# Modulation rounds laid out by column group, and one-pass spreading of the mLSTM maxima, in a two-layer DiT block

## The reference

```
s_lat, s_ctx = silu(c), silu(c_ctx)
for l in (0, 1):                                   # the six modulation vectors of each layer
    mod_lat, mod_ctx = s_lat @ ada_w[l] + ada_b[l], s_ctx @ ada_w[l] + ada_b[l]   # 1024 -> 6144
    h = rms_norm(x, g) * (1 + scale) + shift       # before the mixer and before the network
    x = x + gate * mixer(h); x = x + gate2 * swiglu(h2)
...
# mLSTM, in chunks of 128 tokens, per head and direction:
m_q = max(b + m, rowmax(dmat))                     # a stabilising maximum per query
p   = exp(dmat - m_q[:, None]) * (q @ k.T);  inter = exp(b + m - m_q)
h   = (inter * (q @ S) + p @ v) / max(abs(den), exp(-m_q))
```

## Time and profile before

| | us |
|---|---|
| median of three runs | 1793.11 (1791.22 to 1794.06) |
| the profiled execution | 1791.71 |
| its span, first to last instruction | 1789.9 |
| TensorE busy in the span | 1702.0 (95%) |
| DVE, ACT, POOL busy | 802.6 (45%), 591.5 (33%), 68.2 (4%) |
| mean granted TensorE clock | 0.98 of full speed |

### The profile page before, as it was taken

One profiled execution on the slowest core, in us unless ns is written; L12 is line 12 of the kernel. 1 busy time (PEld: TensorE's weight loads), 2 busy tenths in 40 slices (PEclk: granted clock), 3 DMA queues, 4 the chain that ended last, 5 costly groups with the idle time before them and its releaser, 6 DMA issues.

```text
span 1789.9 us, 26602 instructions
## 1 busy us (share of the span) xinstructions
PE 1702.0 (95%) x10524; PEld 1408.0 (79%) x10524; DVE 802.6 (45%) x1192; ACT 591.5 (33%) x1021; POOL 68.2 (4%) x116
## 2 busy tenths in 40 slices
PE   5999999889899999999999988999998899999998
PEld 4888878668788888888888866777776688888886
DVE  4687777433522222222222455666654533333333
ACT  4344444442421111121112333454664322222221
POOL 0321011000000000000000000000000000000000
PEclk8999999899999999999999998999999999999999
DMA  8532333122122431215221531101113233323233
GB/s 331 60 94 95 130 119 109 50 78 60 46 61 68 166 128 59 68 61 200 94 69 60 207 136 36 47 28 45 36 59 106 70 101 99 94 94 102 91 100 117
DMA packets 47219, 168.99 MB, mean 94 GB/s; under 512 B 5296, under 2 KB 5552, under 8 KB 47024
## 3 DMA queue, kind: packets, MB, share of 16 engines
q1 hardware_dynamic: 31408, 115.47, 19.9%
q10 hardware_dynamic: 14976, 51.52, 7.9%
q0 software_dynamic: 768, 1.08, 0.8%
HBM read 163.82 MB, written 4.19 MB: 94 GB/s over the span
## 4 chain that ended last, share of the span: by engine, by line
PE 88%; ACT 3%; DVE 3%; DMA 3%; issue 1%; ACTq 0%; SPq 0%; DVEq 0%
PE PS L472 52%; PE PS L1842 9%; PE PS L2030 7%; DMA scr<-in_ada 3%; PE PS L1719 3%; PE PS L1885 2%; PE PS L1728 2%; PE PS L1901 1%; PE PS L2118 1%; PE PS L2117 1%; PE PS L1735 1%; PE PS L1781 1%; PE PS L1867 1%; PE PS L1985 1%; PE PS L1795 1%
## 5 line engine op out<-in xcount | busy, mean ns | idle before, releaser
L458 DVE TENSOR_TENSOR w_lo<-raw,w_hi 128x1024 fp32r<-128x1024 f32 x196 | 239.8, 1224 | 254.2 <-ACT w_hi L453 248.5
L472 PE MATMUL PS<-h_hi,w_hi 128*128 128x512 f32 x1008 | 303.8, 355 | 2.6 <-DVE w_lo L458 2.6
L472 PE MATMUL PS<-h_lo,w_hi 128*128 128x512 f32 x1008 | 302.1, 354 | 0.0
L472 PE MATMUL PS<-h_hi,w_lo 128*128 128x512 f32 x1008 | 302.1, 354 | 0.0
L453 ACT ACTIVATE w_hi<-raw 128x1024 fp32r<-128x1024 f32 x196 | 206.3, 1053 | 262.6 <-PE PS L472 218.4
L472 PE MATMUL PS<-c_hi,w_hi 128*128 128x512 f32 (+1 forms) x672 | 204.5, 358 | 4.7 <-DVE w_lo L458 4.7
L472 PE MATMUL PS<-c_hi,w_lo 128*128 128x512 f32 (+1 forms) x672 | 201.9, 354 | 0.0
L472 PE MATMUL PS<-c_lo,w_hi 128*128 128x512 f32 (+1 forms) x672 | 201.7, 354 | 0.0
L472 PEld LDWEIGHTS PS<-h_hi,w_hi 128*128 128x128 f32 x1008 | 165.2, 188 | 30.7 <-DVE w_lo L458 3.3
L472 PEld LDWEIGHTS PS<-h_lo,w_hi 128*128 128x128 f32 x1008 | 165.8, 188 | 28.8
L472 PEld LDWEIGHTS PS<-h_hi,w_lo 128*128 128x128 f32 x1008 | 164.8, 188 | 28.0
(11 more groups left out here) (284 smaller groups left out, 2125.6 us busy)
## 6 DMA issues: line engine op xcount, KB each, us to landing
raw<-in_w SPq DMA_DIRECT2D x196, 512.0 KB, 3.5
scr<-in_ada ACTq DMA_DIRECT2D x48, 512.0 KB, 5.7
adaw<-in_ada ACTq DMA_DIRECT2D x32, 512.0 KB, 4.4
scr<-in_ada SPq DMA_DIRECT2D x8, 1024.0 KB, 10.1
X<-in_xT SPq DMA_DIRECT2D x4, 768.0 KB, 6.8
X<-in_xT ACTq DMA_DIRECT2D x1, 3072.0 KB, 10.2
x_spill<-X ACTq DMA_DIRECT2D x1, 2048.0 KB, 9.3
X<-x_spill ACTq DMA_DIRECT2D x1, 2048.0 KB, 10.0
```

What stands on the lines that cost most here:

```text
L458: nc.vector.tensor_tensor(w_lo[:, j], raw[:, j].rearrange("p (k n) -> p k n", k=KT), w_hi[:, j].bitcast(f32), ALU.subtract).then_inc(s_lo, 1)
L472: last = nc.tensor.matmul(G[j][:, a:b], w[:, j, k], m[:, k, a:b], start=(n == 1), stop=(n == 3 * k_tiles))
```

## The change

The first part is for the rounds of four chunks alone. `ada_four` turns the layout over: chunk q goes to column group q with all its eight input blocks, so the sum over the blocks is finished in PSUM, and a round fills 128 columns of a bank in place of 512. The four chunks take turns matmul by matmul, the input block is the outer loop. ACT copies 128 columns. `ada_turned` is a single f32 matmul: the copied block is the stationary operand, and eight columns of the identity (two of each group of 32) are the moving one. There are 32 matmuls in a round as before.

The second part is the maxima. POOL now rounds `rsel` to `fp32r` (rows 0 to 47 of `rs_r`) and writes the remainder into rows 64 to 111; the rows between are zero. A block of ones with 112 rows, rounded once, is the stationary operand of one `fp32r` matmul of 512 columns, which adds high and low part. The two new tiles lie in columns of `c_hi` and `c_lo` that the second layer doesn't use.

```diff
-        adr_f, at = carve(scr, at, 512)
-        adr_0 = scr[:, 8192:9216].rearrange("p (a n) -> p a n", a=2)
+        adr_f, at = carve(scr, at, 128)
+        adr_0 = scr[:, 8192:8448].rearrange("p (a n) -> p a n", a=2)
...
+        rs_r, ones_r = c_lo[0:112, 6:8, 512:768], c_hi[0:112, 7, 536:664]
...
+            nc.gpsimd.memset(rs_r.bitcast(f32), 0.0).then_inc(s_ones, 1)
+            nc.gpsimd.tensor_copy(ones_r, ones[0:112]).then_inc(s_ones, 1)
+            pool.wait_ge(s_ones, 2)
...
                 nc.gpsimd.tensor_tensor(rsel[0:48].rearrange("p (c i) -> p c i", c=CH), row, pick, ALU.mult)\
-                    .then_inc(s_rs2, 1)
+                    .then_inc(s_rsf, 1)
+                pool.wait_ge(s_rsf, 2 * n + 1)
+                whole = rsel[0:48].rearrange("p (a i) -> p a i", a=2)
+                nc.gpsimd.tensor_copy(rs_r[0:48], whole).then_inc(s_rsf, 1)
+                pool.wait_ge(s_rsf, 2 * n + 2)
+                nc.gpsimd.tensor_tensor(rs_r[64:112], whole, rs_r[0:48].bitcast(f32), ALU.subtract).then_inc(s_rs2, 1)
...
-                    nc.scalar.activation(adr_f, PS[:, 4], ACT.Copy).then_inc(s_adr, 1)
+                    nc.scalar.activation(adr_f, PS[:, 4, 0:128], ACT.Copy).then_inc(s_adr, 1)
...
+            def ada_four(ws, bank):
+                for k in range(KT):
+                    for q, w in enumerate(ws):
+                        last = MM(PS[32 * q:32 * q + 32, bank, 0:128], sT[:, k], w[:, 128 * k:128 * k + 128],
+                                  start=(k == 0), stop=(k == KT - 1))
+                last.then_inc(s_adm, 4)
+
+            def ada_turned(adr, dst):
+                pick = ident.rearrange("p (g r) -> p g r", g=4)[:, :, 0:2]
+                MM(dst.rearrange("p (g s) -> p g s", g=4), adr, pick, start=True, stop=True).then_inc(s_ads, 1)
...
                                 for q in range(4):
                                     pe.wait_ge(s_adf[q], 16 * na + 16)
-                                    ada_row(adaf[:, q], 4, q)
+                                ada_four([adaf[:, q] for q in range(4)], 4)
...
-                                ada_sums(adr_f, ADQ)
+                                ada_turned(adr_f, ADQ)
...
-                MM(PS[:, 5], ones[0:48, :], rsel[0:48], start=True, stop=True).then_inc(s_R, 1)
+                MM(PS[:, 5].rearrange("p (a i) -> p a i", a=2), ones_r, rs_r, start=True, stop=True).then_inc(s_R, 1)
```

More of the change, by code:

```diff
@@ L337, in program @@
         s_gw, s_wgh, s_wgl, s_g1, s_g2 = sem("gatew_loaded"), sem("gatew_hi"), sem("gatew_lo"), sem("gate_pe"), sem("gate_dve")
-        s_g3, s_fn = sem("gate_act"), sem("forget_negated")
+        s_g3, s_fn, s_ones, s_rsf = sem("gate_act"), sem("forget_negated"), sem("ones_rounded"), sem("rsel_step")
         s_pad, s_mcv, s_sil, s_rot, s_rope = sem("padded"), sem("mconv_step"), sem("silu_ready"), sem("rot_done"), sem("rope_step")
@@ L697, in _ @@
                     act.wait_ge(s_ads, n - 1)
-                nc.scalar.activation(adr_0[:, n % 2], PS[:, 6 + n % 2], ACT.Copy).then_inc(s_adr, 1)
+                nc.scalar.activation(adr_0[:, n % 2], PS[:, 6 + n % 2, 0:128], ACT.Copy).then_inc(s_adr, 1)
                 if n == 0:
@@ L1730, in ada_row, with ada_sums @@
                 last.then_inc(s_adm, 1)
-            def ada_sums(adr, dst, nq=4):
-                for q in range(nq):
+            def ada_sums(adr, dst):
+                for q in range(2):
                     last = MM(dst[:, 2 * q:2 * q + 2], adr[:, 128 * q:128 * q + 128], cn("fold"), start=True, stop=True)
                 last.then_inc(s_ads, 1)
+            def ada_four(ws, bank):
[7 more added lines that the diff above has]
+                MM(dst.rearrange("p (g s) -> p g s", g=4), adr, pick, start=True, stop=True).then_inc(s_ads, 1)
             def ffn(layer):
@@ L1818, in _ @@
                     pe.wait_ge(s_adr, n - 1)
-                for q in range(4):
-                    ada_row(scr[:, 1024 * (4 * (n % 2) + q):1024 * (4 * (n % 2) + q) + 1024], 6 + n % 2, q)
+                ada_four([scr[:, 1024 * (4 * (n % 2) + q):1024 * (4 * (n % 2) + q) + 1024] for q in range(4)], 6 + n % 2)
                 if n == 0:
@@ L1825, in _ @@
                 pe.wait_ge(s_adr, n + 1)
-                ada_sums(adr_0[:, n % 2], ADP[n])
+                ada_turned(adr_0[:, n % 2], ADP[n])
                 if n:
@@ L1953, in _ @@
                     pe.wait_ge(s_adr, 4 + U)
-                    ada_sums(adr_m, ADM, 2)
+                    ada_sums(adr_m, ADM)
                 if U < ADA_R:
```

## The result

The changed kernel is slower: 1801.28 us median of nine runs (1795.67 to 1806.96) against 1793.62 for the kernel before (nine runs, 1785.81 to 1794.91), a ratio of 1.0049 with a 95% interval of [1.0035, 1.0063]. By the ratio that is 8.8 us more (the two medians lie 7.7 apart). It is above the range given and near the slow rival (B), though only part of that rival's reason was at work. The profiled execution has a span of 1802.4 us.

A forecast was written before the change was run, and what follows sets the result against it. TensorE was taken as the bound, except in group 2, bound by the loop through the loads. Terms +7.4 + 5.5 - 4.9 - 0.9 - 9.1 + 0.6 (mLSTM clock) = -1.4 gave 1791.7 us, range 1784.5 to 1798.0.

The forecast's parts named there:

- rival (B): Layer 0, group 2: its loop runs cold, every round drops the clock, maxima gain only 5.8; +7.6 us, 1800.7, chance 0.13.
- The waits for four loads: Six late network rounds: all 32 matmuls follow the fourth load's landing, each ending 1.24 us later; +7.4 us.
- The clock behind them: Late network rounds: TensorE idles before the landing and its granted clock falls, 2.7 drops of 2.05 us; +5.5 us.
- The sums: Network rounds: four f32 matmuls become one, saving 0.59 us each, eight on the path in groups 0 and 1; -4.9 us.
- The copy: Start, rounds 1 to 3: ACT's copy of 128 columns, not 512, saves 0.31 us each; -0.9 us.
- The maxima: mLSTM: one fp32r matmul for the f32 one saves 0.65 us at 14 places; -9.1 us.
- POOL: mLSTM: three POOL instructions per unit end in time for TensorE; slowing of DVE put at 0, dear end +3 us.
- The sum: Whole kernel: all terms together give -1.4 us, 1791.7 us against the median; chance 0.44 within about 3 us.

The follow-up runs named there:

- the waits by themselves: Kernel before, changed only so TensorE waits for all four loads of a network round ahead of the first chunk: 1.0043, +7.7 us.
- The version with the waits removed: Kernel before plus column-group rounds, one turning matmul and ACT issuing group 2's next loads earlier; old maxima: 0.9994, -1.1 us.
- The part as a whole: Kernel before with only the new maxima (POOL rounds and subtracts, one fp32r matmul), rounds as before: 1.0004, +0.7 us.
- without POOL's added instructions: Kernel before with the short fp32r maxima matmul, high and low rows formed once and stacked, one POOL instruction per unit: 0.9979, -3.8 us.
- the version with two: Kernel before plus column-group rounds, earlier group 2 loads and the turning matmul issued twice in network rounds; old maxima: 0.9975.
- POOL's work by itself: Kernel before plus all POOL instructions of the new maxima, TensorE keeping the old f32 matmul: 1.0007, +1.3 us.
- the stacked maxima: Kernel before with one fp32r maxima matmul on high and low rows formed once, masked by one POOL instruction per unit: 0.9979, -3.8 us.

## Why the prediction was wrong, step by step

- **The waits for four loads** (+7.4): right in place, number and kind. Six rounds start in one run behind a landing, and the waits by themselves cost 7.7 us, clock included. In that profile the four rounds of group 2 are 4.4 us longer without the clock's share, 1.1 for each, where 1.24 was forecast.
- **The clock behind them** (+5.5, 2.7 drops): too large. In these rounds one drop showed in the changed kernel and two with the waits alone. Both had one behind the 3.5 to 4 us in the first round of group 2, the other was in the first round of group 0, behind 1.9 us; the nine other stretches, of 1.0 to 2.3 us, cost none. Round 4 was forecast to idle 3.1 us and to drop with 0.8; it idled 2.23 and didn't. Over all profiles in which a round waits in this way, the first round of group 2 idled 3.5 to 4.3 us and the clock fell behind 8 of 10; of the 34 other stretches, 0.6 to 2.5 us, it fell behind 4, each of 1.9 us or more. I had also stretched what the Trainium skill says (TensorE: Matmul & The Clock Gate, HAM oscillation): the kernel of that section waits about 3 to 5 us for a DMA before each burst, and here only the first round of group 2 does. (Four drops would be 1.5 more than the 2.5 put down for this group, not 1.3.) Together the first two terms were 12.9 and measured 7.7, in a kernel whose waits in group 2 are some 0.5 us shorter than those of the change.
- **The sums** (-4.9): the step that failed. Their own saving was under-sized if anything, 0.67 us each. But I took the products around them as fixed, and one f32 matmul in place of four put these at the slow pace: +7.8 us by the pairs. Sum and pace together are about +2 and not -4.9. The traces agree: from the first round of group 0 to that of group 2 TensorE's work at full clock is 388.6 us before and 389.5 in the changed kernel, where -4.7 was forecast. The version with the waits removed shows it too: it should have been some 6 us faster than before, and was 1.1.
- **The copy** (-0.9): where it was said to be, and near its size. From the end of a round's rows to the product behind it 2.91 us pass before and 2.58 in the changed kernel, in the third and the fourth round. The copy is shorter by 0.32 (0.28 in place of 0.60), so nothing of this comes from the shorter sums. The first whole projection begins at 62.5 us in the changed kernel and at 63.9 in the one before, and at 62.2 and 63.8 in the mean of the ten profiles with the new rounds at the start and of the seven without; what is beyond three times 0.32 isn't the copy. In the two profiles the clock also comes back earlier under the first product, which lasts 5.9 us in place of 7.0 (from 31.09 and from 30.73 us).
- **The maxima** (-9.1): the other step that failed, by more us, and in two ways. The saving was over-sized: 0.65 us at 14 places, from one pair of rows, where TensorE's work fell by about 6 us in all, as in half of the units the f32 maxima had been interleaved with the matmuls behind it. The rest was eaten by what I put at 0, **POOL** beside DVE. The part as a whole is at +0.7, and without POOL's added instructions at -3.8, so these take about 4.5 back (the two intervals overlap slightly). In the traces 1.9 of it is the one wait at the first outputs. The rest would be clock: over their runs the three kernels with these instructions and the short matmul have a mean granted clock of 0.975 to 0.976, all other versions 0.977 to 0.980; that this comes from the wait isn't shown. I had looked whether POOL ends in time for TensorE, and it does; I had not looked at what DVE does at that moment, which was the last thing ahead of the first outputs, with less than 1 us to spare before. The Trainium skill (GPSIMD Engine Reference, Key points) has this rule, that POOL contends with DVE instructions on two SBUF inputs; the trace agrees, with 1.53 us for one of 0.68.
- **The sum**: +7.7 for the waits, +7.8 for the pace, -6 for nine sums on the path (eight in groups 0 and 1 and the last), -1.4 at the start and +0.7 for the maxima make +8.8. That this meets the measured number to the tenth is luck, as the measured terms are known to 2 or 3 us each. The forecast of -1.4 had the two large gains without what each did to its neighbours. Rival (B) gave 1800.7, near the time, by five clock drops in these rounds of which one came in the profile; it was right by accident.

What stays open: why the parity of f32 matmuls between the products (whether their number is odd or even) sets the pace. Each is two records with two weight loads in the trace, so it isn't the parity of records; the median weight load takes 188 ns at either pace. Products of 512 columns alone, in layer 1, have one pace (0.2267) in every profile. Open too is why the clock falls behind the first outputs with POOL's added instructions, even behind a wait of 0.16 us.

## What to carry to other kernels

When an edit merges waits, look at what used to run between them: work that filled a wait costs nothing there, and moving it behind the last arrival puts it on the path and leaves the engine idle. When an edit gives a side engine more to do, look at what the engine that it can slow does at that moment, which of the two starts first, and how much slack there is to the next wait. When a row gives the cost of an instruction, look at more than one place before multiplying it. And measure a long stream's pace per matmul before and after: a small instruction between products changed it here by 1.9%, at full clock, with no wait to be seen in any list.

## What the runs showed of the hardware

- A stream of `fp32r` matmuls that alternates 512 and 256 columns has two paces, 0.3467 and 0.3533 us for a pair, at a granted clock of 1.00. Behind 1, 3 or 5 f32 matmuls in each iteration it was the slow one, behind 2 or 4 the fast one (the first product behind a change can still have the old pace: 8.58 us, then 8.43, in the version with two).
- An f32 matmul with a 128 x 128 stationary operand and 8 moving columns takes 0.14 to 0.22 us in a stream, with 2 columns 0.20.
- An f32 matmul of 48 x 512 has its follower 0.96 us behind it, or has the next matmuls between its two records; the same in `fp32r` has it 0.32 to 0.44 us behind.
- A DVE instruction with two SBUF operands of 512 columns beside a POOL instruction took 1.53 us in place of 0.68, and the POOL copy beside DVE 2.09 in place of 0.61. In the overlaps that I looked at (the changed kernel, POOL's work by itself, the stacked maxima) the instruction that started second took 0.2 to 1.5 us longer, the one that started first at most 0.4.
